# RWKV-7 delta-rule scan on one core: the sixth level of the triangular inverse on its 64x64 corner, in two row halves of the array, with one direction's key transposes in front of each half

## The chip, the cores and the metric

One core of a Trainium2 chip runs the whole kernel. The metric is device time in microseconds (us), the median over runs; lower is better. Times of single instructions come from one profiled execution.

## The reference

Two blocks of a network run in sequence over x of 1024 tokens and width 1024. The change lies in the first block's RWKV-7 branch: a gated delta rule, 16 heads of width 64, run forwards and backwards over 256 context tokens and 1024 tokens. Cut to what matters:

```python
def rwkv7_scan(r, w, k, v, kk, a, S0, reverse):
    def step(S, inp):
        sa = jnp.einsum('bhvk,bhk->bhv', S, kk_t)
        S = (S * w_t[:, :, None, :] - sa[..., None] * b_t[:, :, None, :]
             + v_t[..., None] * k_t[:, :, None, :])
        o = jnp.einsum('bhvk,bhk->bhv', S, inp[5])
        return S, o
    S, o = lax.scan(step, S0, xs, reverse=reverse)
...
    for d in (0, 1):                      # forwards and backwards
        S, o = rwkv7_scan(rh, w, kd, vh, kk, a, S0[d], reverse=(d == 1))
    o = head_norm((outs[0] + outs[1]), ln_w, ln_b, A_HEADS, A_GN_EPS) + bonus
    return ((o * silu(g)) @ w_o), states
```

## The kernel before

The function `rwkv` does the scan in chunks of 128 tokens. One chunk of one head needs the inverse of a 128x128 unit triangular matrix (the tokens of a chunk depend on one another through the keys). The work is cut into units `(i, n)`: `i` is one of 8 pairs of heads, `n` one of 5 pairs of chunks, so there are 40 units. A unit holds two directions, `x = 0` (forwards) and `x = 1` (backwards), and for each 4 matrices `q` (2 heads by 2 chunks). The four matrices of a direction lie side by side in one PSUM bank; direction `x` has banks `4x` to `4x+3`, `bank(x, 0)` to `bank(x, 3)`.

The inverse is built in levels. Y holds the inverse so far, block diagonal with blocks of 2^m after level m-1, and E the matrix that takes part in making the next factor. Level m of a direction:

- TensorE: `f` multiplies E by G (result F, in `bank(x, 0)`), and `ey` multiplies G by E and Y together (a moving operand of 256 columns, result in banks 1 and 2).
- VectorE: `join` takes F, multiplies it by the mask `lev{m}` and leaves the next G.
- ScalarE copies two of the four results of `ey` back to SBUF (`low{m}`), and the other two (`high{m}`) for x = 0; for x = 1 VectorE copies the `high{m}` ones.

Levels 1 to 4 are so done. Level 5 needs no new E: `f` makes F5 and `y_next` (`Y5`) makes the new Y alone, 128 columns wide. Level 6, the last, is `y_next` again (`Y6`) with G6 from F5. Its result lies only in a 64x64 corner of each 128x128 matrix, since the diagonal blocks of 64 are done by then: for x = 0 rows 0 to 63 and columns 64 to 127, for x = 1 the opposite corner. ScalarE copies Y5 and Y6 back (`y_out`, L1220).

Behind the levels of a unit the order on TensorE is written out by hand, and the next unit's front is interleaved with it: `turn_kv` (transposes of the next unit's keys and values, 4 instructions for each direction, L1299 and L1301, into `bank(x, 1)`; it waits for `low4`), `Y6`, `turn_ab` (4 transposes for each direction, L1310 and L1312, into `bank(x, 0)`; it waits for G6), `solve` (C0 = Y times the right side, L1347 on `b_Rr`; it waits for Y6's copy), `gram_b` (L1320 on `b_Bt`; it waits for `Btok`, ScalarE's copy of the transposes, L1201), `product` (L1347 on `b_C`), `gram_k` (L1320 on `b_Kt`), `refine` (L1347 on `b_G,b_EY`, eight in a row), `start` (L1338, L1341) and so on. `gram_b` and `gram_k` contract over 64 partitions only: their instructions go in turn to the upper and the lower 64 rows of the array, which the profile writes as `64*128`.

On ScalarE the copies stand in an order of their own, in which each waits for its turn: Y5 (x = 0, 1), the four copies of the keys and values (`keys_out`, L1195), Y6 (x = 0, 1), then `pairs_out` (L1200, L1201) and `solved` (L1224) of x = 0, and the same of x = 1.

Of the kernel before, what the change touches and what calls it, by code (L numbers as in the profile page):

```python
# [18 lines left out]
ALU = mybir.AluOpType  # L19
ACT = mybir.ActivationFunctionType  # L20
# [933 lines left out]
def rwkv(nc, G, proj, Xd, oa, v_tok, rope):  # L954
# [15 lines left out]
    with nc.cleanup_on_exit(), ExitStack() as ctx:  # L970
# [39 lines left out]
        by_head = lambda t: t.rearrange("p (t h c) -> p h t c", t=2, h=2)  # L1010
        spare = lambda h: bank(h, 3)
        both = lambda x: ps[:, 4 * x + 1:4 * x + 3].rearrange("p b (q a f) -> p (b q) a f", q=2, a=2)

# [9 lines left out]
        def level_names(n, x):  # L1023
            return {"pe": ["F0", "E0"] + sum(([f"F{m}", f"EY{m}"] for m in range(1, 5)), []) + ["F5", "Y5", "Y6"],
                    "act": ["E0"] + sum(([f"low{m}"] + ([] if high_on_dve(x) else [f"high{m}"]) for m in range(1, 5)), []) + ["Y5", "Y6"],
                    "dve": ["G0", "G1"] + sum(([f"G{m}"] + ([f"high{m - 1}"] if high_on_dve(x) and m < LEVELS - 1 else []) for m in range(2, LEVELS)), [])}
# [30 lines left out]
        with nc.Block() as block:  # L1057
# [124 lines left out]
            def _(act):  # L1182
# [34 lines left out]

                def y_out(i, n, x, m):
                    L[x]["pe"].wait(act, i, f"{n}.Y{m}")
                    L[x]["act"].done(A(Y[x], heads(x, 2), ACT.Copy), f"{n}.Y{m}")  # L1220

# [16 lines left out]
                for i, n in UNITS_B:  # L1238
                    nxt = after(i, n)
                    for m in range(1, 5):  # L1240
                        for x in range(2):
                            ey_out(i, n, x, m)
                    for x in range(2):
                        y_out(i, n, x, 5)
                    if nxt:
                        for x in range(2):
                            keys_out(*nxt, x)
                    for x in range(2):
                        y_out(i, n, x, last)
                    for x in range(2):  # L1250
# [19 lines left out]
            def _(pe):  # L1270
# [106 lines left out]

                def y_next(i, n, x, m):
                    L[x]["dve"].wait(pe, i, f"{n}.G{m}")
                    if m == 6:  # L1380
                        L[x]["act"].wait(pe, i, f"{n}.Y5")
                    L[x]["pe"].done(quad(bank(x, 2), Gs[x][m % 2], Y[x]), f"{n}.Y{m}")

                def levels(i, n):
                    for m in range(1, 6):
                        for x in range(2):
                            f(i, n, x, m)
                            if m < 5:
                                ey(i, n, x, m)
                            else:  # L1390
                                y_next(i, n, x, m)
                        if m == 1 and i and n == 0:
                            mean(i - 1)
                        if m == 1 and i and n == 1:
                            for x in range(2):
                                B[x]["dve"].wait(pe, i, "0.QT")
                            variance(i - 1)

                def solve(i, n, x):
# [86 lines left out]
                for i, n in UNITS_B:  # L1486
                    nxt = after(i, n)
                    levels(i, n)
                    if nxt:
                        turn_kv(*nxt, 0)  # L1490
                        turn_kv(*nxt, 1)
                    for x in range(2):
                        y_next(i, n, x, last)
                        if nxt:
                            turn_ab(*nxt, x)
# [26 lines left out]
            def _(dve):  # L1522
# [53 lines left out]
                def join(i, n, x, m):  # L1576
                    if m == 0:
                        F[x]["pe"].wait(dve, i, f"{n}.XT")
                    else:
                        L[x]["pe"].wait(dve, i, f"{n}.F{m - 1}")  # L1580
                    L[x]["dve"].done(V.tensor_tensor(Gs[x][m % 2][:], heads(x, 0 if m else 1), rep(K(f"lev{m}"), 4), ALU.mult), f"{n}.G{m}")  # L1581

# [1895 lines left out]
```

How the kernel before makes its waits and increments, by code:

```python
    def wait(self, back=0):  # L68
        self.eng.wait_ge(self.sem, self.it * self.per + (self.base + self.n - back))
# [48 lines left out]
    def load(self, eng, src, i, per, l, split=False):  # L118
        if split:
            eng.wait_ge(self.cut, i * per + (self.split_base + l + 1))
        else:
            eng.wait_ge(self.free, i * per + (self.base - self.split_base + l + 1))
        b = (self.base + l) % NBUF
        eng.dma_start(self.buf[:, b], src).then_inc(self.full[b], 16)
# [1 line left out]
    def landed(self, eng, i, per, l):  # L127
        n = self.base + l
        eng.wait_ge(self.full[n % NBUF], i * (16 * per // NBUF) + 16 * (n // NBUF + 1))
        return self.buf[:, n % NBUF]
# [1 line left out]
    def split_hi(self, act, l):  # L133
        n = self.split_base + l
        raw = self.landed(act, 0, 0, l)
        act.wait_ge(self.begun, n + 1)
        self.nc.scalar.activation(self.hl[:, n % NBUF, 0], raw, ACT.Copy).then_inc(self.hi_done, 1)
# [1 line left out]
    def split_lo(self, dve, l):  # L140
        n = self.split_base + l
        hi, lo = self.hl[:, n % NBUF, 0], self.hl[:, n % NBUF, 1]
        dve.wait_ge(self.hi_done, n + 1)
        self.nc.vector.tensor_tensor(lo, self.buf[:, (self.base + l) % NBUF], hi.bitcast(F32), ALU.subtract).then_inc(self.cut, 1)
# [1 line left out]
    def split_first(self, eng, scalar):  # L147
# [6 lines left out]
            self.nc.scalar.activation(hi, raw, ACT.Copy).then_inc(self.hi_done, 1)  # L154
        else:
            eng.wait_ge(self.hi_done, n + 1)
            self.nc.vector.tensor_tensor(lo, raw, hi.bitcast(F32), ALU.subtract).then_inc(self.cut, 1)
```

## Time and profile before

| | |
|---|---|
| time, median of 3 runs | 4689.36 us (4686.57 to 4690.65) |
| the profiled execution | 4687.34 us, of which 4685.6 us span from the first to the last instruction |
| TensorE matmuls | busy 4531.5 us (97%) |
| TensorE weight loads | busy 3671.8 us (78%) |
| VectorE | busy 2674.1 us (57%) |
| ScalarE | busy 1728.0 us (37%) |
| GpSimd | busy 457.7 us (10%) |
| granted TensorE clock, mean | 0.986 of 2.4 GHz |

Busy time counts an instruction from start to end, and the ends of matmuls overlap the next ones' starts: a matmul of 0.28 us can be followed by the next after 0.11 us. So what a group of matmuls costs is read from the start of the group to the start of the next group, not from its busy time. The scan's 40 units lie between 1373 and 2609 us of the span. In every unit the stretch that the change touches looks alike in the trace, so one unit is shown (i = 3, n = 2).

### The profile page before, as it was taken

The page shows a single profiled execution, that of the slowest core. Times are in us where ns is not written, and L with a number is a line of the kernel's source. Part 1 is how long each engine was busy: PE and PEld are TensorE (multiplying, and loading weights), DVE is VectorE, ACT ScalarE, POOL GpSimd, SP SyncE. Part 2 cuts the span into 40 slices and gives each one's busy share as a digit, 9 for nine tenths or more (in the row PEclk, how much of TensorE's full clock was granted, in tenths as well). Part 3 has the DMA queues.
Part 4 walks back from the last instruction along what each step waited for, and adds up shares of the span by engine and source line. Part 5 has one row for each costly group of instructions (what it writes and reads, how often), then busy time and mean ns, then how long its engine had stood idle before and what let it go on. Part 6 is the DMA issues. An engine that isn't in the chain of part 4 may idle for free. (4 is left out here: it accounts for less than half of the span.)

```text
span 4685.6 us, 66517 instructions
## 1 busy us (share of the span) xinstructions
PE 4531.5 (97%) x27608; PEld 3671.8 (78%) x27608; DVE 2674.1 (57%) x3938; ACT 1728.0 (37%) x2924; POOL 457.7 (10%) x371
## 2 busy tenths in 40 slices
PE   7999999999999999999999799899998789999999
PEld 4888877778999888988898444688777567888887
DVE  3245544555636676767677676546453755555543
ACT  3234444444424544554445343211343742111111
POOL 0000000000012233322334100000010000000000
PEclk8999999999999999999999999999999999999999
DMA  5244343434430110111012343333120021212222
GB/s 207 99 144 148 134 144 138 145 139 148 160 115 15 45 57 30 59 45 59 28 59 86 90 150 120 128 107 134 54 71 15 23 113 59 72 68 77 99 90 95
DMA packets 155978, 441.79 MB, mean 94 GB/s; under 512 B 17168, under 2 KB 47120, under 8 KB 140448
## 3 DMA queue, kind: packets, MB, share of 16 engines
q1 hardware_dynamic: 140624, 383.98, 23.5%
q0 software_dynamic: 9296, 32.58, 2.0%
q10 hardware_dynamic: 5760, 20.97, 1.2%
q8 instruction: 221, 3.62, 0.3%
q14 instruction: 77, 0.63, 0.0%
HBM read 294.86 MB, written 141.56 MB: 93 GB/s over the span
## 5 line engine op out<-in xcount | busy, mean ns | idle before, releaser
L202 PE MATMUL pr_ps<-uhl,w_split 128*128 128x512 f32 (+1 forms) x1520 | 586.9, 386 | 3.1 <-DVE w_split L145 2.2
L206 PE MATMUL pr_ps<-uhl,w_split 128*128 128x512 f32 (+1 forms) x1520 | 571.7, 376 | 0.0
L205 PE MATMUL pr_ps<-uhl,w_split 128*128 128x512 f32 (+1 forms) x1520 | 571.1, 376 | 0.0
L1581 DVE TENSOR_TENSOR b_G<-b_ps,cst 128x512 fp32r<-128x512 f32 x560 | 383.2, 689 | 95.4 <-PE b_ps L1361 93.7
L138 ACT ACTIVATE w_split<-share 128x2048 fp32r<-128x2048 f32 x64 | 122.6, 1916 | 698.9 <-DVE ou_vc L3303 271.1
L202 PEld LDWEIGHTS pr_ps<-uhl,w_split 128*128 128x128 f32 x1520 | 287.0, 189 | 81.7 <-issue 29.2
L205 PEld LDWEIGHTS pr_ps<-uhl,w_split 128*128 128x128 f32 x1520 | 287.3, 189 | 56.3 <-issue 5.8
L206 PEld LDWEIGHTS pr_ps<-uhl,w_split 128*128 128x128 f32 x1520 | 286.9, 189 | 52.8
L1124 POOL TENSOR_SCALAR b_Mr<-b_tri 128x512 fp32r<-128x512 f32 x80 | 117.8, 1490 | 1908.7 <-DVE b_tri L1565 1908.7
L202 PE MATMUL ou_ps<-ou_a,w_split 128*128 128x512 f32 x704 | 276.5, 393 | 7.7 <-DVE ou_a L2158 7.7
L1361 PE MATMUL b_ps<-b_G,b_EY 128*128 128x128 f32 x1600 | 275.4, 281 | 0.0
L206 PE MATMUL ou_ps<-ou_a,w_split 128*128 128x512 f32 x704 | 274.5, 390 | 0.0
L205 PE MATMUL ou_ps<-ou_a,w_split 128*128 128x512 f32 x704 | 274.5, 390 | 0.0
L776 DVE COPY pr_stage<-pr_ps 128x256 f32<-128x256 f32 (+1 forms) x92 | 49.7, 540 | 393.4 <-PE pr_ps L206 393.2
L1214 ACT ACTIVATE b_EY<-b_ps 128x512 fp32r<-128x512 f32 x320 | 192.1, 600 | 217.4 <-PE b_ps L1375 217.4
L202 PE MATMUL mx_ps<-mx_a,w_split 128*128 128x512 f32 x640 | 259.1, 405 | 13.5 <-DVE mx_a L2158 13.5
L205 PE MATMUL mx_ps<-mx_a,w_split 128*128 128x512 f32 x640 | 254.1, 397 | 0.0
L206 PE MATMUL mx_ps<-mx_a,w_split 128*128 128x512 f32 x640 | 253.9, 397 | 0.0
L1361 PEld LDWEIGHTS b_ps<-b_G,b_EY 128*128 128x128 f32 x1600 | 222.2, 189 | 36.8 <-issue 12.0
L202 PE MATMUL ou_ps<-ou_ext,w_split 128*128 128x512 f32 x576 | 224.1, 389 | 0.0
L205 PE MATMUL ou_ps<-ou_ext,w_split 128*128 128x512 f32 x576 | 224.1, 389 | 0.0
L206 PE MATMUL ou_ps<-ou_ext,w_split 128*128 128x512 f32 x576 | 224.1, 389 | 0.0
(498 smaller groups left out, 10030.2 us busy)
## 6 DMA issues: line engine op xcount, KB each, us to landing
w_ring<-in_w_in SPq DMA_DIRECT2D x41, 1024.0 KB, 5.3
proj<-pr_stage SPq DMA_DIRECT2D x160, 256.0 KB, 2.0
share<-in_w_up SPq DMA_DIRECT2D x24, 1024.0 KB, 4.8
ar<-share SPq DMA_DIRECT2D x32, 512.0 KB, 2.8
b_AR<-ar SPq DMA_DIRECT2D x64, 256.0 KB, 2.9
pr_raw<-proj SPq DMA_DIRECT2D x48, 256.5 KB, 3.5
ada<-in_ada_w SPq DMA_DIRECT2D x24, 512.0 KB, 5.6
ff<-ou_vc ACTq DMA_DIRECT2D x24, 512.0 KB, 2.6
```

The lines of the kernel that those rows point to most:

```text
L138: self.nc.scalar.activation(self.hl[:, n % NBUF, 0], raw, ACT.Copy).then_inc(self.hi_done, 1)
L202: mm = nc.tensor.matmul(dst, a[0], b[0], start=start, stop=False)
L205: nc.tensor.matmul(dst, a[0], b[1], start=False, stop=False)
L206: return nc.tensor.matmul(dst, a[1], b[0], start=False, stop=stop)
L776: V.tensor_copy(dst, src).then_inc(taken[1], 1)
L1124: F[x]["pool"].done(ts(Mr[x][:], tri[x][e][:], 1.0, None, ALU.mult), f"{n}.Mr")
L1214: L[x]["act"].done(A(EY[x][:, 0:2], both(x)[:, 0:2], ACT.Copy), f"{n}.low{m}")
L1361: mm = mmul(bank(x, 0)[:, q * P:(q + 1) * P], E[x][:, q] if m else Mr[x][:, q], Gs[x][m % 2][:, q], start=True, stop=True)
L1581: L[x]["dve"].done(V.tensor_tensor(Gs[x][m % 2][:], heads(x, 0 if m else 1), rep(K(f"lev{m}"), 4), ALU.mult), f"{n}.G{m}")
```

## The change

- Level 5's `f` no longer runs over the whole matrices. `y_five` makes Y5 for both directions first; then `corner_f` makes the corner of F5 alone: for each matrix a 64-row contraction, weights of 64 rows by 128 columns, moving operand of 64 rows by 64 columns. It alternates between the directions, and direction 0 lies in the upper 64 rows of the array (partitions), direction 1 in the lower.
- VectorE's last `join` becomes a multiplication by -1 of the 64x64 corners (64 partitions by 256 elements in place of 128 by 512), without the mask.
- `corner_y` takes the place of Y6: again 64-row contractions with 64 moving columns that alternate between the directions, now 0 in the lower rows and 1 in the upper. It begins with a wait for G6 and Y5's copy of both directions. ScalarE copies back the 64x64 corners alone (`corner_out`).
- `turn_kv` of x = 0 moves ahead of Y5, and `turn_kv` of x = 1 stands between `corner_f` and `corner_y`. The `turn_ab` of both directions stand behind `corner_y`, where x = 0's stood between the two Y6. On ScalarE `keys_out` is moved in the same way: x = 0's ahead of the Y5 copies, x = 1's behind them.
- The waits for `low4` and `high4` of a direction, which F5 had, are now those of its Y5; `turn_kv` has its wait for `low4` as before.

```diff
--- before.py
+++ after.py
@@ -1009,6 +1009,9 @@
         heads = lambda x, b: ps[:, 4 * x + b].rearrange("p (q f) -> p q f", q=4)
         by_head = lambda t: t.rearrange("p (t h c) -> p h t c", t=2, h=2)
         spare = lambda h: bank(h, 3)
+        edge = [slice(64, P), slice(0, 64)]
+        rest = [slice(0, 64), slice(64, P)]
+        corners = lambda x, b: bank(x, b)[:, 0:256].rearrange("p (q f) -> p q f", q=4)
         both = lambda x: ps[:, 4 * x + 1:4 * x + 3].rearrange("p b (q a f) -> p (b q) a f", q=2, a=2)
 
         last = LEVELS - 1
@@ -1021,7 +1024,7 @@
         high_on_dve = lambda x: x == 1
 
         def level_names(n, x):
-            return {"pe": ["F0", "E0"] + sum(([f"F{m}", f"EY{m}"] for m in range(1, 5)), []) + ["F5", "Y5", "Y6"],
+            return {"pe": ["F0", "E0"] + sum(([f"F{m}", f"EY{m}"] for m in range(1, 5)), []) + ["Y5", "F5", "Y6"],
                     "act": ["E0"] + sum(([f"low{m}"] + ([] if high_on_dve(x) else [f"high{m}"]) for m in range(1, 5)), []) + ["Y5", "Y6"],
                     "dve": ["G0", "G1"] + sum(([f"G{m}"] + ([f"high{m - 1}"] if high_on_dve(x) and m < LEVELS - 1 else []) for m in range(2, LEVELS)), [])}
 
@@ -1215,9 +1218,13 @@
                     if not high_on_dve(x):
                         L[x]["act"].done(A(EY[x][:, 2:4], both(x)[:, 2:4], ACT.Copy), f"{n}.high{m}")
 
-                def y_out(i, n, x, m):
-                    L[x]["pe"].wait(act, i, f"{n}.Y{m}")
-                    L[x]["act"].done(A(Y[x], heads(x, 2), ACT.Copy), f"{n}.Y{m}")
+                def y_out(i, n, x):
+                    L[x]["pe"].wait(act, i, f"{n}.Y5")
+                    L[x]["act"].done(A(Y[x], heads(x, 2), ACT.Copy), f"{n}.Y5")
+
+                def corner_out(i, n, x):
+                    L[x]["pe"].wait(act, i, f"{n}.Y6")
+                    L[x]["act"].done(A(Y[x][rest[x], :, edge[x]], corners(x, 2)[rest[x]], ACT.Copy), f"{n}.Y6")
 
                 def solved(i, n, x):
                     B[x]["pe"].wait(act, i, f"{n}.C0")
@@ -1240,13 +1247,14 @@
                     for m in range(1, 5):
                         for x in range(2):
                             ey_out(i, n, x, m)
+                    if nxt:
+                        keys_out(*nxt, 0)
                     for x in range(2):
-                        y_out(i, n, x, 5)
+                        y_out(i, n, x)
                     if nxt:
-                        for x in range(2):
-                            keys_out(*nxt, x)
+                        keys_out(*nxt, 1)
                     for x in range(2):
-                        y_out(i, n, x, last)
+                        corner_out(i, n, x)
                     for x in range(2):
                         if nxt:
                             pairs_out(*nxt, x)
@@ -1375,26 +1383,45 @@
                         mm = mmul(both(x)[:, q], Gs[x][m % 2][:, q], EY[x][:, q], start=True, stop=True)
                     L[x]["pe"].done(mm, f"{n}.EY{m}")
 
-                def y_next(i, n, x, m):
-                    L[x]["dve"].wait(pe, i, f"{n}.G{m}")
-                    if m == 6:
+                def y_five(i, n, x):
+                    L[x]["dve"].wait(pe, i, f"{n}.G5")
+                    L[x]["act"].wait(pe, i, f"{n}.low4")
+                    high(x).wait(pe, i, f"{n}.high4")
+                    L[x]["pe"].done(quad(bank(x, 2), Gs[x][1], Y[x]), f"{n}.Y5")
+
+                def corner_f(i, n):
+                    for q in range(4):
+                        for x in range(2):
+                            mm = mmul(corners(x, 0)[:, q], E[x][rest[x], q], Gs[x][1][rest[x], q, rest[x]], start=True, stop=True)
+                            if q == 3:
+                                L[x]["pe"].done(mm, f"{n}.F5")
+
+                def corner_y(i, n):
+                    for x in range(2):
+                        L[x]["dve"].wait(pe, i, f"{n}.G6")
                         L[x]["act"].wait(pe, i, f"{n}.Y5")
-                    L[x]["pe"].done(quad(bank(x, 2), Gs[x][m % 2], Y[x]), f"{n}.Y{m}")
+                    for q in range(4):
+                        for x in range(2):
+                            mm = mmul(corners(x, 2)[:, q], Gs[x][0][edge[x], q], Y[x][edge[x], q, edge[x]], start=True, stop=True)
+                            if q == 3:
+                                L[x]["pe"].done(mm, f"{n}.Y6")
 
                 def levels(i, n):
-                    for m in range(1, 6):
+                    for m in range(1, 5):
                         for x in range(2):
                             f(i, n, x, m)
-                            if m < 5:
-                                ey(i, n, x, m)
-                            else:
-                                y_next(i, n, x, m)
+                            ey(i, n, x, m)
                         if m == 1 and i and n == 0:
                             mean(i - 1)
                         if m == 1 and i and n == 1:
                             for x in range(2):
                                 B[x]["dve"].wait(pe, i, "0.QT")
                             variance(i - 1)
+                    for x in range(2):
+                        if x == 0 and after(i, n):
+                            turn_kv(*after(i, n), 0)
+                        y_five(i, n, x)
+                    corner_f(i, n)
 
                 def solve(i, n, x):
                     i_, n_ = before(i, n)
@@ -1487,11 +1514,10 @@
                     nxt = after(i, n)
                     levels(i, n)
                     if nxt:
-                        turn_kv(*nxt, 0)
                         turn_kv(*nxt, 1)
-                    for x in range(2):
-                        y_next(i, n, x, last)
-                        if nxt:
+                    corner_y(i, n)
+                    if nxt:
+                        for x in range(2):
                             turn_ab(*nxt, x)
                     solve(i, n, 0)
                     solve(i, n, 1)
@@ -1578,6 +1604,9 @@
                         F[x]["pe"].wait(dve, i, f"{n}.XT")
                     else:
                         L[x]["pe"].wait(dve, i, f"{n}.F{m - 1}")
+                    if m == last:
+                        L[x]["dve"].done(V.tensor_scalar(Gs[x][0][edge[x], :, rest[x]], corners(x, 0)[edge[x]], -1.0, None, ALU.mult), f"{n}.G{m}")
+                        return
                     L[x]["dve"].done(V.tensor_tensor(Gs[x][m % 2][:], heads(x, 0 if m else 1), rep(K(f"lev{m}"), 4), ALU.mult), f"{n}.G{m}")
 
                 def high_out(i, n, x, m):
```

TensorE's order behind the last `ey` (level 4) of a unit, the first one, before. `b_G` and `b_EY` hold G, and E with Y; `cst` is the identity of the transposes, `share` the memory in which this unit's keys lie; `128x128` is the moving operand's shape and x4 the count.

```order
L1375 MATMUL b_ps<-b_EY,b_G 128x256 x4
L1361 MATMUL b_ps<-b_G,b_EY 128x128 x4
L1347 MATMUL b_ps<-b_EY,b_G 128x128 x4
L1361 MATMUL b_ps<-b_G,b_EY 128x128 x4
L1347 MATMUL b_ps<-b_EY,b_G 128x128 x4
L1299 MATMUL b_ps<-cst,share 128x128 x2
...
L1347 MATMUL b_ps<-b_EY,b_G 128x128 x4
L1310 MATMUL b_ps<-cst,share 128x128 x2
L1312 MATMUL b_ps<-cst,share 128x128 x2
L1347 MATMUL b_ps<-b_EY,b_G 128x128 x4
```

The same place of the changed kernel, the lines with its own numbers (L1307 and L1309 are `turn_kv`, L1355 Y5, L1395 `corner_f`, L1405 `corner_y`, L1318 and L1320 `turn_ab`).

```order
L1383 MATMUL b_ps<-b_EY,b_G 128x256 x4
L1307 MATMUL b_ps<-cst,share 128x128 x2
L1309 MATMUL b_ps<-cst,share 128x128 x2
L1355 MATMUL b_ps<-b_EY,b_G 128x128 x8
L1395 MATMUL b_ps<-b_G,b_EY 128x64 x8
L1307 MATMUL b_ps<-cst,share 128x128 x2
L1309 MATMUL b_ps<-cst,share 128x128 x2
L1405 MATMUL b_ps<-b_EY,b_G 128x64 x8
L1318 MATMUL b_ps<-cst,b_AR 128x128 x2
L1320 MATMUL b_ps<-cst,share 128x128 x2
```

The eight instructions of F5 and the eight of Y6 became eight of 64 columns each, a group of transposes now stands ahead of Y5 and one between the two corner groups, and both `turn_ab` follow `corner_y`.

ScalarE's copies from level 4's last `low4` to the first `solved`, before:

```order
L1214 ACTIVATE b_EY<-b_ps 128x512
L1220 ACTIVATE b_EY<-b_ps 128x4x128 x2
L1195 ACTIVATE b_KV<-b_ps 128x256 x4
L1220 ACTIVATE b_EY<-b_ps 128x4x128 x2
L1200 ACTIVATE b_AM<-b_ps 128x4x64
L1201 ACTIVATE b_MB<-b_ps 128x4x64
L1224 ACTIVATE b_C<-b_ps 128x512
```

And now (L1217 is `low4`, L1223 Y5's copy, L1227 the corner's):

```order
L1217 ACTIVATE b_EY<-b_ps 128x512
L1198 ACTIVATE b_KV<-b_ps 128x256 x2
L1223 ACTIVATE b_EY<-b_ps 128x4x128 x2
L1198 ACTIVATE b_KV<-b_ps 128x256 x2
L1227 ACTIVATE b_EY<-b_ps 64x4x64 x2
L1203 ACTIVATE b_AM<-b_ps 128x4x64
L1204 ACTIVATE b_MB<-b_ps 128x4x64
L1231 ACTIVATE b_C<-b_ps 128x512
```

Two of the four key copies moved ahead of the Y5 copies, and the last pair of Y copies became smaller.

## Rows read from the trace of the kernel before

**Rows 1.** The scan's window: us; PE, PEld, DVE, ACT, POOL busy; PEclk; DMA; GB/s.

```profile
1373.20:2609.40 1236.20, 1231.32 (x12216) 1109.45 (x12216) 866.37 (x1621) 589.19 (x1252) 408.84 (x284) 1.00 0.14 48
```

**Rows 2.** Timeline of TensorE's matmuls in one unit: start, length, line, count.

```profile
1912.14 0.84 PE L1361 MATMUL b_ps<-b_G,b_EY 128*128 128x128 f32 x4
1912.81 0.61 PE L1347 MATMUL b_ps<-b_EY,b_G 128*128 128x128 f32 x4
1913.26 0.61 PE L1361 MATMUL b_ps<-b_G,b_EY 128*128 128x128 f32 x4
1913.70 0.61 PE L1347 MATMUL b_ps<-b_EY,b_G 128*128 128x128 f32 x4
1914.15 0.41 PE L1299 MATMUL b_ps<-cst,b_Kt 128*128 128x128 f32 x2
...
1914.97 0.64 PE L1347 MATMUL b_ps<-b_EY,b_G 128*128 128x128 f32 x4
...
1916.68 1.13 PE L1347 MATMUL b_ps<-b_Rr,b_EY 128*128 128x128 f32 x8
1917.74 2.14 PE L1320 MATMUL b_ps<-b_AR,b_Bt 64*128 64x256 f32 x16
1919.81 2.05 PE L1347 MATMUL b_ps<-b_C,b_tri 128*128 128x128 f32 x16
1921.79 2.00 PE L1320 MATMUL b_ps<-b_AR,b_Kt 64*128 64x256 f32 x16
1923.72 1.11 PE L1347 MATMUL b_ps<-b_G,b_EY 128*128 128x128 f32 x8
1924.66 0.39 PE L1338 MATMUL b_ps<-b_ident_r,b_Mr 128*128 128x128 f32 x2
```

**Rows 3.** Timeline of ScalarE in the same unit.

```profile
1911.89 0.59 ACT L1216 ACTIVATE b_EY<-b_ps 128x512 fp32r<-128x512 f32 x1
1912.37 0.60 ACT L1214 ACTIVATE b_EY<-b_ps 128x512 fp32r<-128x512 f32 x1
...
1914.85 1.21 ACT L1195 ACTIVATE b_KV<-b_ps 128x256 f32<-128x256 f32 x4
1915.90 1.20 ACT L1220 ACTIVATE b_EY<-b_ps 128x512 fp32r<-128x512 f32 x2
...
1917.53 0.62 ACT L1224 ACTIVATE b_C<-b_ps 128x512 f32<-128x512 f32 x1
...
1918.27 0.43 ACT L1201 ACTIVATE b_MB<-b_ps 128x256 f32<-128x256 f32 x1
```

**Rows 4.** Timeline of VectorE: the end of the same unit's levels.

```profile
1912.40 0.68 DVE L1585 CAST b_EY<-b_ps 128x512 fp32r<-128x512 f32 x1
1913.01 0.69 DVE L1581 TENSOR_TENSOR b_G<-b_ps,cst 128x512 fp32r<-128x512 f32 x1
1913.90 0.69 DVE L1581 TENSOR_TENSOR b_G<-b_ps,cst 128x512 fp32r<-128x512 f32 x1 [0.20 <-PE b_ps L1361]
```

**Rows 5.** Timeline of VectorE later in the unit: two operations of 256 elements.

```profile
1925.38 0.41 DVE L1593 TENSOR_TENSOR b_WN<-b_C,b_ps 128x256 f32<-128x256 f32 x1
1925.70 0.42 DVE L1594 SCALAR_TENSOR_TENSOR b_WN<-b_ps,b_C 128x256 f32<-128x256 f32 x1
```

**Rows 6.** Timeline of VectorE in the unit before: operations of 64 elements.

```profile
1901.01 0.48 DVE L1607 TENSOR_SCALAR b_S<-b_ps,b_dmp 128x64 f32<-128x64 f32 x2 [1.02 <-PE b_ps L1462]
```

**Rows 7.** Timeline of weight loads: half-array ones, 1917.74 to 1917.86.

```profile
1917.74 0.30 PEld L1320 LDWEIGHTS b_ps<-b_AR,b_Bt 64*128 64x128 f32 x4
```

**Rows 8.** Timeline of weight loads: whole-array ones, and the one that waited.

```profile
1913.20 0.53 PEld L1361 LDWEIGHTS b_ps<-b_G,b_EY 128*128 128x128 f32 x4
...
1918.74 0.73 PEld L1320 LDWEIGHTS b_ps<-b_AR,b_Bt 64*128 64x128 f32 x8 [0.27 <-ACT b_MB L1201]
```

**Rows 9.** Groups by line in the scan: count, busy us, mean ns of one.

```profile
L1220 ACT ACTIVATE b_EY<-b_ps 128x512 fp32r<-128x512 f32 x160 | 95.8, 609 | 31.5 <-PE b_ps L1347 31.5
...
L1446 PE MATMUL b_ps<-b_WN,b_MB 128*64 128x64 f32 x576 | 37.5, 222 | 0.0
```

## The prediction

> **What bounds the kernel now.** I read the window of the scan first: in 1236.2 us TensorE's matmuls are busy for 1231.3 us, at a granted clock of 1.00 (2.4 GHz), while VectorE is busy for 866 and ScalarE for 589 [rows 1]. So the scan goes at TensorE's pace, and what a unit loses or gains between the starts of TensorE's groups is the kernel's loss or gain. ScalarE makes two Y5 and two Y6 copies a unit, 160 in all, so there are 40 units [rows 9]; 39 of them have a next unit whose transposes are interleaved.
>
> Then the timeline of TensorE. F5 of x = 0 starts at 1912.14, F5 of x = 1 at 1913.26, and each Y5 and the second F5 take 0.44 to 0.45 us from start to start, 0.11 us for a matmul. The first F5 took 0.67: 0.22 us of waiting. The eight transposes of both `turn_kv` take 1914.15 to 1914.97 = 0.82 us (0.41 for a direction; the `turn_ab` are of the same kind), and `solve` starts at 1916.68 [rows 2]. From F5 to `solve` a unit spends 4.54 us, all of it touched by the change.
>
> Two more waits lie behind. `gram_b` of x = 1 waited: its weight load at 1918.74 had a hole of 0.27 us before it and follows ScalarE's `Btok`, which ended at 1918.27 + 0.43 = 1918.70 [rows 3, 8]. Its price: `gram_b` takes 1917.74 to 1919.81 = 2.07 us and `gram_k`, the same work without the wait, 1921.79 to 1923.72 = 1.93, so 0.14. And `solve` takes 1.06 us to the next start, where `refine`, eight matmuls too, takes 0.94 [rows 2]; of the 0.12, some 0.09 are the switch to half-array instructions (below), and 0.03 a wait for Y6's copy of x = 1, which ended at 1915.90 + 1.20 = 1917.10 [rows 3]. Both waits are ScalarE's queue being late.
>
> **What the parts cost.** Removed: 16 whole-array matmuls, 16 x 0.11 = 1.78 us. Added: 16 half-array ones. G, E and Y are fp32r, as the copies that write them show [rows 3, 4]; the half-array instructions of the trace work on plain f32. So I bound the price of a pair (one in each half). The half-array weight loads of `gram_b`: four, two for each half, take 0.30 us in all [rows 7], where four whole-array loads take 0.53 [rows 8]. With 0.19 for the length of one, that is 0.11 from pair to pair against 0.11 from load to load. So the halves load side by side, and a pair costs 0.11 us if the weights set the pace; if the halves took turns in this format it would be 0.22. I take 0.11, since the load has the same 128 columns: four pairs in 0.44 us where eight matmuls took 0.89.
>
> Switches. The change goes from whole to half and back twice more in each unit. `product`, 16 whole-array matmuls, takes 1.98 us to `gram_k` against 16 x 0.1115 = 1.78, so 0.20 for the switch with the first load laid bare; `refine` takes 0.94 against 0.89, so 0.05 for a bare first load in the scan's number format, with no switch behind it [rows 2]. Left for the switch itself: 0.10 to 0.15; I take 0.10, hence 0.15 with the load. Above the row the Trainium skill ("TensorEngine Tiling (Array Packing)", Key Properties) speaks against this change: changing the tiling mode drains the array. The trace agrees, with those 0.10 us; were a switch free, the two that lie on the path here would give back 2 x 0.15 x 39 = 12 us more than I forecast.
>
> Handovers: a copy starts 0.03 us after the recorded end of the matmul (F5 of x = 1 ends at 1913.26 + 0.61 = 1913.87, VectorE starts at 1913.90 [rows 2, 4]); a weight load follows a copy by 0.05 (1918.70 to 1918.74 [rows 3, 8]).
>
> **The new sequence**, in the times of this unit:
> - `turn_kv` of x = 0 starts at 1912.14 and ends its slot at 1912.55. It fills the wait that F5 had: `high4` of x = 0 ends at 1911.89 + 0.59 = 1912.48 [rows 3], so Y5 of x = 0 loads at 1912.53 and is through at 1912.53 + 0.05 + 0.45 = 1913.03.
> - Y5 of x = 1 now needs `high4` of x = 1, VectorE's copy of 1912.40 + 0.68 = 1913.08 [rows 4]. Before, that was hidden behind Y5 of x = 0. It loads at 1913.13: a new wait of 0.10 and a bare load of 0.05. Its slot ends at 1913.63.
> - Switch: `corner_f` loads at 1913.73; its fourth pair starts at 1913.73 + 0.05 + 3 x 0.11 = 1914.11 and its record ends 0.22 later (a matmul of 64 columns, [rows 9]), at 1914.33.
> - VectorE makes G6 of x = 0 from 1914.36. 256 elements for each partition take 0.41, the next begins 0.33 later [rows 5]: x = 1 ends at 1914.36 + 0.33 + 0.41 = 1915.10. Below this lies the row of 64 elements, two in 0.48 [rows 6]: 1914.84; above it the full-length 0.69 with 0.61 between starts [rows 4]: 1915.66.
> - Meanwhile `turn_kv` of x = 1 runs and ends at about 1914.75, so 0.3 us of TensorE lie idle, and both switches around the transposes are hidden in them.
> - `corner_y` loads at 1915.15, its fourth pair starts at 1915.53. ScalarE's queue isn't what it waits for: the keys' copies of x = 0 start when `low4` of x = 1 is through (1912.97), take 0.27 each, and two Y5 copies of 0.6 end by 1914.6.
> - Switch, bare load, 0.82 us of `turn_ab`: 1915.53 + 0.05 (its own 64 columns, an estimate) + 0.15 + 0.80 (0.82 less the bare load that is counted already) = 1916.53 is `solve`'s start. Before it was 1916.68: **0.15 us gained.**
> - ScalarE has the two corner copies (256 elements: 0.4 each, 0.27 apart, as the keys' copies: four in 1.21 [rows 3]) from 1915.78 to 1916.45, not 1917.10. So `solve` of x = 1 finds Y6 there: **0.03 gained.** The first C0 copy, which started at 1917.53 because the queue was late, starts when its matmuls are through: 1916.53 + 0.03 + 0.33 + 0.28 + 0.03 = 1917.20. `Btok` of x = 1, which ended 1.17 after that start, ends at 1918.37, while `gram_b` now starts at 1917.74 - 0.18 = 1917.56 and asks for it at about 1918.40 (half of `gram_k`'s 1.93 less one load of 0.11 after its start): **0.14 gained.**
>
> Nothing further behind loses it again: VectorE's masks and GpSimd's copies start from `gram_b` and move with it. Sum: 0.32 us a unit, 39 x 0.32 = 12.5 us. The last unit has no transposes to fill the wait for G6 and loses an estimated 0.5. Total 12.0: the profiled execution would come to 4687.3 - 12.0 = 4675.3, and the median, 2.0 above it, to 4689.4 - 12.0 = **4677.4 us**.
>
> So the 0.9 us of matmul time taken away come to 0.32, since the path now runs through Y5, a switch, the corner, VectorE and the second corner.
>
> **The rivals.**
> - *The halves take turns (slower).* A pair costs 0.22 in this number format; both corner groups are on the path, each 0.44 longer. Against it: the loads of [rows 7] overlap. For it: all half-array instructions of the trace are of the other format. The unit then changes by +0.88 - 0.32 = +0.56, 39 of them +22 us, with the last one 4712. It decides where a pair costs over 0.15 (8 pairs x 0.04 = 0.32).
> - *Something on the new path costs a little more (no change to be seen).* The two bare switches at 0.15 instead of 0.10, or semaphores that take 0.05 longer at three places, or the wait for `high4` longer: 0.2 us a unit, 8 us. For it: the path is a chain of seven handovers, each priced from other places. 4685.
> - *G6 full length.* VectorE's price doesn't follow the elements: 0.56 later, 39 x 0.56 = 22 us, 4699. Against it: 0.41 for 256 elements in [rows 5].
> - *G6 short, or pairs quicker.* By [rows 6] G6 ends 0.26 sooner: -10 us, 4667. TensorE would then have no idle time left, so more isn't to be had there.
>
> **How the numbers follow.** Forecast (4671 to 4683) 0.60; a little more costly 0.18; halves in turn 0.10; full-length G6 0.03; short 0.09. About 0.2% (9.4 us) is what a measurement of this kernel tells from no change, so faster begins at 4680. Of the forecast's case three quarters are below that (0.45), and all of the short one (0.09): faster 0.54. Same: 0.15 and 0.16 of the second case, 0.31. Slower: 0.10 + 0.03 + 0.02 = 0.15. The range reaches from the short G6 with a little more, 4665, to the full-length one, 4699; only the halves in turn are outside.
>
> **What would show it.** From the first `turn_kv` to `solve` 4.4 us in a unit, not 4.5; weight loads of `corner_f` in pairs 0.01 apart and 0.11 from pair to pair; a hole of some 0.3 us before `corner_y` that VectorE's G6 ends; no hole before `gram_b` of x = 1; the 40 units' window 12 us shorter. I am wrong if the pairs start 0.1 apart, if ScalarE's Y5 copy ends the wait of `corner_y`, or if the wait before `gram_b` is still there.

## The result, and the profile after

The changed kernel takes **4731.02 us** (median of 5 runs, 4721.81 to 4734.12) against 4686.57 (4685.37 to 4690.65) before, where two runs more have joined the three of the table: a ratio of 1.0091, 95% interval 1.0079 to 1.0103. It is slower by 44 us, where 12 us faster was forecast, and it lies outside the range. The profiled execution of the changed kernel took 4721.81 us with a span of 4720.0. It is the fastest of the five, so the profile shows the loss at its mildest.

The busy times of the whole page show nothing of this:

```profile
PE 4543.8 (96%) x27608; PEld 3672.3 (78%) x27608; DVE 2657.5 (56%) x3938; ACT 1719.6 (36%) x2924; POOL 458.1 (10%) x371
```

One stretch inside the scan does. The columns are those of [rows 1]; the first row is the kernel before, the second the changed one, in fences of their own.

```profile
1400.00:2580.00 1180.00, 1175.83 (x11672) 1059.18 (x11671) 828.54 (x1549) 564.21 (x1201) 384.75 (x266) 1.00 0.14 48
```

```profile
1400.00:2580.00 1180.00, 1155.40 (x11317) 1026.72 (x11313) 787.76 (x1502) 540.66 (x1165) 357.67 (x248) 0.97 0.14 46
```

The reader is to see two things. The granted clock is 0.97, where it was 1.00: 3% of 1180 us are some 35 us. And TensorE is idle for 25 us of the stretch, where it was idle for 4. Windows of 5 us in the changed kernel show where the clock went:

```profile
1405.00:1410.00 5.00, 5.00 (x39) 4.66 (x40) 4.54 (x8) 3.49 (x7) 0.00 (x0) 1.00 0.01 3
1410.00:1415.00 5.00, 4.42 (x43) 3.85 (x41) 2.49 (x5) 3.77 (x9) 0.00 (x0) 0.98 0.00 0
1415.00:1420.00 5.00, 5.00 (x25) 4.63 (x26) 0.00 (x0) 3.05 (x8) 0.00 (x0) 0.50 0.02 3
1420.00:1425.00 5.00, 5.00 (x38) 4.11 (x36) 3.88 (x6) 0.00 (x0) 2.98 (x2) 0.83 0.00 0
```

The second window holds an idle time of 0.58 us (4.42 of 5.00 busy). Behind it the clock is at 0.50, the lower of its two levels (1.2 GHz), comes back in the fourth window and is 1.00 until it falls again some units later (0.50 in 1545 to 1550). The timeline of TensorE around the same place, columns as in [rows 2]:

```profile
1413.42 0.38 PE L1309 MATMUL b_ps<-cst,share 128*128 128x128 f32 x2
1414.38 0.66 PE L1405 MATMUL b_ps<-b_EY,b_G 64*128 64x64 f32 x8 [0.58 <-DVE b_G L1608]
1414.97 0.69 PE L1318 MATMUL b_ps<-cst,b_AR 128*128 128x128 f32 x2
1415.45 0.64 PE L1320 MATMUL b_ps<-cst,share 128*128 128x128 f32 x2
...
1416.59 1.95 PE L1355 MATMUL b_ps<-b_Rr,b_EY 128*128 128x128 f32 x8
```

The pairs of `corner_y` (L1405) still go nearly at full speed; the transposes behind them take 0.64 for two instead of 0.38, and `solve` 1.95 instead of 1.09. The hole is the wait for G6, VectorE's two copies of F5's corner. It is there in every unit, and the clock falls behind about every fourth of them: ten times in the stretch, each time within 1 us of the end of a hole.

Apart from the clock, the path is no shorter either. A unit with its clock at 1.00, from `solve` to `solve`, takes 31.57 us before (from 1916.68 [rows 2]) and 31.70 after (from 1931.94, below). Two of every five units are shorter (30.89 and 29.83 before), and they too are 0.13 longer now. The next `solve` in the timeline of the kernel before, and in that of the changed one:

```profile
1948.25 1.14 PE L1347 MATMUL b_ps<-b_Rr,b_EY 128*128 128x128 f32 x8
```

```profile
1963.64 1.09 PE L1355 MATMUL b_ps<-b_Rr,b_EY 128*128 128x128 f32 x8
```

The timeline of the changed kernel's TensorE over such a unit's end:

```profile
1927.08 0.41 PE L1307 MATMUL b_ps<-cst,b_Kt 128*128 128x128 f32 x2
1927.33 0.38 PE L1309 MATMUL b_ps<-cst,b_V 128*128 128x128 f32 x2
1927.57 1.23 PE L1355 MATMUL b_ps<-b_EY,b_G 128*128 128x128 f32 x8
1928.73 0.63 PE L1395 MATMUL b_ps<-b_G,b_EY 64*128 64x64 f32 x8
1929.30 0.44 PE L1307 MATMUL b_ps<-cst,b_Kt 128*128 128x128 f32 x2
1929.57 0.38 PE L1309 MATMUL b_ps<-cst,b_V 128*128 128x128 f32 x2
1930.53 0.63 PE L1405 MATMUL b_ps<-b_EY,b_G 64*128 64x64 f32 x8 [0.58 <-DVE b_G L1608]
1931.10 0.44 PE L1318 MATMUL b_ps<-cst,b_AR 128*128 128x128 f32 x2
...
1931.94 1.09 PE L1355 MATMUL b_ps<-b_Rr,b_EY 128*128 128x128 f32 x8
1932.96 2.00 PE L1328 MATMUL b_ps<-b_AR,b_Bt 64*128 64x256 f32 x16
1934.89 2.05 PE L1355 MATMUL b_ps<-b_C,b_tri 128*128 128x128 f32 x16
```

From the first `turn_kv` to `solve` it takes 4.86 us; the stretch from F5 to `solve` that it answers to took 4.54 [rows 2], and 4.39 was forecast. `gram_b` now takes 1.93 (1932.96 to 1934.89), not 2.07: the wait before its x = 1 is gone, as forecast.

### The profile page after: what moved, and what is told of

It reads as the page before. It is cut to its first block and busy times, and to the rows that moved or that the text cites. A ratio compares the mean times of both kernels' runs of the same rounds, so it can differ in the third digit from the quotient of the medians.

```text
span 4720.0 us, 66517 instructions
## 1 busy us (share of the span) xinstructions
PE 4543.8 (96%) x27608; PEld 3672.3 (78%) x27608; DVE 2657.5 (56%) x3938; ACT 1719.6 (36%) x2924; POOL 458.1 (10%) x371
## 5 line engine op out<-in xcount | busy, mean ns | idle before, releaser
L1610 DVE TENSOR_TENSOR b_G<-b_ps,cst 128x512 fp32r<-128x512 f32 x480 | 328.0, 689 | 87.2 <-PE b_ps L1369 85.7
L1217 ACT ACTIVATE b_EY<-b_ps 128x512 fp32r<-128x512 f32 x320 | 192.4, 601 | 217.4 <-PE b_ps L1383 217.4
L1383 PE MATMUL b_ps<-b_EY,b_G 128*128 128x256 f32 x1280 | 220.1, 293 | 0.0
L1369 PE MATMUL b_ps<-b_G,b_EY 128*128 128x128 f32 x1280 | 217.6, 280 | 0.0
```

The lines of the kernel that those rows point to most:

```text
L1217: L[x]["act"].done(A(EY[x][:, 0:2], both(x)[:, 0:2], ACT.Copy), f"{n}.low{m}")
L1369: mm = mmul(bank(x, 0)[:, q * P:(q + 1) * P], E[x][:, q] if m else Mr[x][:, q], Gs[x][m % 2][:, q], start=True, stop=True)
L1383: mm = mmul(both(x)[:, q], Gs[x][m % 2][:, q], EY[x][:, q], start=True, stop=True)
```

## The experiments

Each edit is against the changed kernel. The clock is that of the stretch 1400 to 2580, the unit that of the timeline at full clock. The kernel before had medians of 4685.16, 4686.32 and 4686.65 us beside the three sets of runs.

**`fill_t`: the hole filled.** Four more transposes stand in front of `corner_y`, into a bank that is free there. They are extra work that nothing uses. Theory A: the clock falls because TensorE idles before `corner_y`. Theory B: it falls for another reason, the half-array instructions for one.

```diff
                         turn_kv(*nxt, 1)
+                        F[0]["act"].wait(pe, nxt[0], f"{nxt[1]}.Vtok")
+                        for q in range(4):
+                            tp(bank(0, 1)[:, q * P:(q + 1) * P], Kt[i % 2][0][:, (at(0, n) + q % 2) * P:(at(0, n) + q % 2 + 1) * P], K("ident"))
                     corner_y(i, n)
```

> Four more key transposes (whole array, results unused) stand in the wait before corner_y, 0.43 us of work in a hole of 0.58 us, off the path. Theory H (the clock falls because TensorE stands still for 0.6 us in every unit): the hole shrinks to 0.15 us, the scan's granted clock goes from 0.97 to 1.00, and the time falls by some 30 to 38 us, to 4692 to 4700. Theory W (what counts is real multiplying work; transposes and 64-column half-array instructions are too thin): the clock stays at 0.97 and the time within 10 us of the changed kernel's 4731. Theory M (all of the loss is mis-sized steps of the path, no clock): same time, 4731, too.

Measured: 4695.73 us, 1.0022 [1.0013, 1.0032]; clock 1.00; unit 31.70, so the extra work lengthened nothing. The clock is back and with it 35 us; the hole left is 0.14 us. A stands against B, though the added work could matter as well as the closed hole.

```profile
1400.00:2580.00 1180.00, 1170.94 (x11776) 1044.31 (x11777) 805.62 (x1538) 554.88 (x1197) 379.45 (x263) 1.00 0.14 48
```

**`fill_m`, `fill_f`: other work in the hole.** The same place; first four fp32r matmuls of E and G5 (`fill_m`), then two f32 matmuls with the identity, each of which is two instructions in the trace (`fill_f`). Unused work too, behind the same wait as in `fill_t`.

```diff
+                        for q in range(4):
+                            mmul(bank(0, 1)[:, q * P:(q + 1) * P], E[0][:, q], Gs[0][1][:, q], start=True, stop=True)
```

```diff
+                        for q in range(2):
+                            mmul(bank(0, 1)[:, q * P:(q + 1) * P], K("ident"), Kt[i % 2][0][:, (at(0, n) + q) * P:(at(0, n) + q + 1) * P], start=True, stop=True)
```

> The same place and length, but four real whole-array fp32r matmuls of 128 columns (E times G5, results unused) in place of the transposes. H and W both: clock back to 1.00 in the scan and 4692 to 4700. Where fill_t stays slow and this one doesn't, W holds against H. M: 4731.

> The hole before corner_y filled as in fill_t and fill_m, now with two real whole-array f32 matmuls (identity times the keys), four instructions of 0.11 us. fill_t's transposes of f32 data kept the clock up (4695.7), fill_m's fp32r matmuls only in part (4707.3). If f32 operands are what keeps the array busy enough: as fill_t, 4692 to 4698. If transposing is: as fill_m, 4703 to 4712.

Measured: `fill_m` 4707.3, 1.0053 [1.0038, 1.0068], unit 31.70, clock 0.99, fallen at some four places; `fill_f` 4696.6, 1.0021 [1.0011, 1.0031], 31.70, clock 1.00.

```profile
1400.00:2580.00 1180.00, 1170.04 (x11684) 1047.19 (x11685) 799.84 (x1527) 550.66 (x1187) 376.56 (x260) 0.99 0.14 48
```

TensorE is as busy here (1170.04 us) as with the transposes (1170.94), and the clock is not held as well. So idle time alone seems not to be the whole rule: what fills the hole counts too. It is not that transposes count more, since plain f32 matmuls hold the clock as they do. One difference besides the number format is left: the hole that remains is 0.18 us in `fill_m`, 0.14 in `fill_t` and 0.13 in `fill_f`. No run separates the two.

**`kv_late`: the transposes of both directions between the corners.**

```diff
                     for x in range(2):
-                        if x == 0 and after(i, n):
-                            turn_kv(*after(i, n), 0)
                         y_five(i, n, x)
...
                     if nxt:
+                        turn_kv(*nxt, 0)
                         turn_kv(*nxt, 1)
```

ScalarE's `keys_out` of x = 0 moves behind the Y5 copies in the same way (not shown).

> Both directions' key transposes stand between corner_f and corner_y, as they stood before Y6 in the kernel before; nothing ahead of Y5. Y5 of x = 0 waits 0.4 us for its last copy instead, but the path (high4 of x = 1, Y5, corner_f, G6, corner_y) is the same: units of 31.70 us where the clock is full. The hole before corner_y shrinks from 0.58 to 0.15. If the clock falls by the thin stretch behind Y5 alone: clock 1.00, 4692 to 4700. If it goes by idle time wherever it lies in the unit: 4721 to 4734.

Measured: 4694.28, 1.0017 [1.0008, 1.0026]; unit 31.70; clock 1.00. The stretch, and TensorE's timeline:

```profile
1400.00:2580.00 1180.00, 1158.10 (x11607) 1028.95 (x11602) 806.49 (x1539) 561.36 (x1197) 380.56 (x263) 1.00 0.14 48
```

```profile
1910.22 1.23 PE L1354 MATMUL b_ps<-b_EY,b_G 128*128 128x128 f32 x8 [0.35 <-ACT b_EY L1219]
1911.39 0.63 PE L1394 MATMUL b_ps<-b_G,b_EY 64*128 64x64 f32 x8
...
1913.18 0.63 PE L1404 MATMUL b_ps<-b_EY,b_G 64*128 64x64 f32 x8
1914.60 1.09 PE L1354 MATMUL b_ps<-b_Rr,b_EY 128*128 128x128 f32 x8
```

This is the cleanest comparison of the study: the same instructions, the same path (31.70), no added work. Of the hole of 0.58, 0.35 now lie before Y5 and 0.14 before `corner_y`. TensorE is idle for 22 us of the stretch, hardly less than the changed kernel's 25 and more than `fill_m`'s 10, and yet the clock holds. The 37 us from here to the changed kernel (4731.0 less 4694.3) are the clock's; the 8 us from the kernel before to here are the path's, as far as the units show it (0.13 us each). To fill the wait before Y5 with transposes, as the changed kernel does, brings nothing on the path: the unit is 31.70 either way.

**`kv_late_hole`: a hole put back.** The edit of `kv_late`, and on top of it VectorE makes G6 of x = 0 twice, first into a scratch tile that nothing reads.

```diff
                     if m == last:
+                        if x == 0:
+                            V.tensor_scalar(scr[edge[x]], corners(x, 0)[edge[x]], -1.0, None, ALU.mult)
```

> kv_late (4694.3, clock 1.00) with one more VectorE operation ahead of G6 of x = 0: it reads the corner once more into a spare tile, so that G6 of both comes about 0.45 us later and the hole before corner_y grows from 0.15 to about 0.6 us, as in the changed kernel, but with both groups of transposes in front of the hole. Path: 0.4 to 0.45 us a unit, 16 to 18 us, 4710 to 4712. If a hole of 0.6 us beside half-array work brings the clock down: 25 to 35 us more, 4735 to 4747. If the transposes' place is what mattered: 4710 to 4712 and the clock stays.

Measured: 4707.9, 1.0047 [1.0032, 1.0062]; unit 32.05; clock 1.00.

```profile
1919.77 1.24 PE L1355 MATMUL b_ps<-b_EY,b_G 128*128 128x128 f32 x8 [0.35 <-ACT b_EY L1220]
...
1923.08 0.63 PE L1405 MATMUL b_ps<-b_EY,b_G 64*128 64x64 f32 x8 [0.48 <-DVE b_G L1609]
```

Two holes, together 0.83 us a unit, more than the 0.58 of the changed kernel, and the clock holds. The sum of the idle time in a unit does not decide. Here a single hole of 0.48 does not let it fall; one of 0.58 in the changed kernel does. That the length makes this difference is not shown: the transposes of both directions stand in front of the hole here, those of one direction there, and no run has this order with a hole of 0.58.

**`order`: the change's order alone, level 6 on the whole array.**

```diff
                 def corner_f(i, n):
-                    for q in range(4):
-                        for x in range(2):
-                            mm = mmul(corners(x, 0)[:, q], E[x][rest[x], q], Gs[x][1][rest[x], q, rest[x]], start=True, stop=True)
-                            if q == 3:
-                                L[x]["pe"].done(mm, f"{n}.F5")
+                    for x in range(2):
+                        L[x]["pe"].done(quad(bank(x, 0), E[x], Gs[x][1]), f"{n}.F5")
```

and so for `corner_y`, `join` (with its mask again) and the copy of Y6 (not shown).

> The change's order alone: F5 and Y6 over the whole matrices, VectorE's and ScalarE's last steps full length, transposes and waits where the change puts them. Path by the rows: Y5, F5 x = 0 and x = 1, G6 of x = 1 full length (0.69), Y6: solve 0.2 to 0.4 us later than before, 4695 to 4702. H: the hole before Y6 is at most 0.2 us, clock 1.00. W: whole-array work, clock 1.00. M: the same. A time near 4731 would say that the order alone, not the corner, brings the clock down.

Measured: 4719.1, 1.0074 [1.0057, 1.009]; unit 32.32; clock 1.00.

```profile
1926.29 1.08 PE L1355 MATMUL b_ps<-b_EY,b_G 128*128 128x128 f32 x8 [0.68 <-DVE b_G L1601]
```

So the order costs 0.75 us a unit (32.32 against 31.57), and the corners give back 0.62 (31.70): the corners are worth having, the order isn't. And with a hole of 0.68, longer than the changed kernel's, the clock holds. How long a hole the clock bears depends on more than its length; what differs here are the instructions around it.

**`order_hole`: `order` with a longer hole**, by an extra, unused VectorE operation ahead of G6 of x = 0.

```diff
+                    if m == last and x == 0:
+                        V.tensor_scalar(scr[:], heads(x, 0)[:, :, 0:64], -1.0, None, ALU.mult)
                     L[x]["dve"].done(V.tensor_tensor(Gs[x][m % 2][:], heads(x, 0 if m else 1), rep(K(f"lev{m}"), 4), ALU.mult), f"{n}.G{m}")
```

> order (4719.1, clock 1.00 in the levels, hole of 0.68 us before Y6, all whole-array work) with one more VectorE operation of 256 elements ahead of G6: the hole grows to 1.0 to 1.1 us. Path: 0.33 to 0.45 us a unit, 13 to 18 us, 4732 to 4737. If idle time alone decides above some length between 0.6 and 1 us: clock falls, 4757 to 4772. If half-array work is needed for it: 4732 to 4737.

Measured: 4775.34, 1.0187 [1.0164, 1.0209]; unit 32.66 where the clock is full, 34.4 where it fell, which is in most units; clock 0.96.

```profile
1445.90 0.38 PE L1310 MATMUL b_ps<-cst,share 128*128 128x128 f32 x2
1447.29 1.58 PE L1356 MATMUL b_ps<-b_EY,b_G 128*128 128x128 f32 x8 [1.01 <-DVE b_G L1604]
1448.67 0.65 PE L1319 MATMUL b_ps<-cst,b_AR 128*128 128x128 f32 x2
```

With 1.01 us of idle time the whole-array order loses its clock too. Half-array instructions are not needed for a fall.

**`wide`: half-array corners with 128 moving columns** instead of 64, in `corner_f` and in `corner_y`; the half of each product that isn't needed is not used.

```diff
-                            mm = mmul(corners(x, 0)[:, q], E[x][rest[x], q], Gs[x][1][rest[x], q, rest[x]], start=True, stop=True)
+                            mm = mmul(heads(x, 0)[:, q], E[x][rest[x], q], Gs[x][1][rest[x], q], start=True, stop=True)
```

> corner_f and corner_y with 128 moving columns in place of 64, still in the two row halves; the copies read the same corners. The weight loads set the pace (0.11 us a pair), so the path and the hole of 0.58 us stay. Theory C (the clock falls because the stretch around the hole streams too few columns; the order run kept its clock with a hole of 0.68 us and whole-array work): clock back to 1.00 for most of the scan, 4692 to 4705. Theory R (half of the rows idle is what counts, or hole and half rows together): columns don't help, 4721 to 4734.

Measured: 4715.28, 1.0062 [1.0047, 1.0077]; unit 31.75; clock 0.99, fallen at five or six places.

```profile
1926.17 0.66 PE L1405 MATMUL b_ps<-b_EY,b_G 64*128 64x128 f32 x8 [0.58 <-DVE b_G L1608]
```

The same hole of 0.58, twice the columns around it, and the clock falls about half as often. Twice the columns cost 0.05 us a unit: a pair is paced by its weight loads, not by its columns.

**`g6_act`: G6 of x = 1 on ScalarE**, so that the two copies of F5's corner run side by side.

```diff
+                def corner_neg(i, n, x):
+                    L[x]["pe"].wait(act, i, f"{n}.F5")
+                    L[x]["act"].done(A(Gs[x][0][edge[x], :, rest[x]], corners(x, 0)[edge[x]], ACT.Copy, scale=-1.0), f"{n}.G6")
...
-                        L[x]["dve"].wait(pe, i, f"{n}.G6")
-                        L[x]["act"].wait(pe, i, f"{n}.Y5")
+                        L[x]["act"].wait(pe, i, f"{n}.G6" if x else f"{n}.Y5")
+                    L[0]["dve"].wait(pe, i, f"{n}.G6")
```

The edit has a second part: `corner_y` now has three waits instead of four, and the one for VectorE's G6 stands last.

> G6 of x = 1 is made by ScalarE, beside VectorE's G6 of x = 0, and corner_y waits for three semaphores instead of four. The step from corner_f to corner_y loses VectorE's second copy (0.46 us) and one wait (0.05): the hole shrinks from 0.58 to about 0.1, a unit gets 0.45 to 0.5 us shorter: 18 to 20 us. H: the clock returns as well, 31 to 38 us more, in all 4673 to 4682, faster than the kernel before. W: work per time rises only a little, the clock stays low in part: 4690 to 4713. M: 4711.

Measured: **4672.75, 0.9973 [0.9962, 0.9983]**; unit 31.14; clock 1.00. The stretch, and the timeline of VectorE, ScalarE and the weight load at that place:

```profile
1400.00:2580.00 1180.00, 1175.69 (x11858) 1047.16 (x11857) 807.88 (x1532) 576.45 (x1253) 395.58 (x275) 1.00 0.14 48
```

```profile
1905.42 0.43 DVE L1615 TENSOR_SCALAR b_G<-b_ps 64x256 fp32r<-64x256 f32 x1 [1.38 <-PE b_ps L1400]
1905.45 0.38 ACT L1227 ACTIVATE b_G<-b_ps 64x256 fp32r<-64x256 f32 x1
...
1905.96 0.33 PEld L1410 LDWEIGHTS b_ps<-b_EY,b_G 64*128 64x128 f32 x4 [0.23 <-issue]
```

Both copies run within 0.43 us; `corner_y` starts 0.54 after the first of them, not 1.10. Of these 0.56 us, 0.45 are the copies side by side (they end at 1905.85, 0.43 after the first one's start and not 0.88) and 0.11 the handover (the load follows by 0.11, not 0.22), which the waits bring, as the next experiment shows. TensorE's order and work are those of the changed kernel here, with nothing added; only the hole before `corner_y` is closed, to 0.02 us, and the clock is back. Of the 58 us to the changed kernel, 0.56 us a unit are 22, and the 36 that remain agree with the 37 of `kv_late`. The version is faster than the kernel before by 0.27% and has both the shorter path and the clock.

**`waits`, `fewer_waits`: the semaphore waits.** `waits` is `fill_t` with the two waits for Y5 ahead of the two for G6. `fewer_waits` is `g6_act` with one of the three waits taken from each Y5, one that another wait on the same semaphore covers: `low4` for x = 0, G5 for x = 1.

```diff
                     for x in range(2):
-                        L[x]["dve"].wait(pe, i, f"{n}.G6")
                         L[x]["act"].wait(pe, i, f"{n}.Y5")
+                    for x in range(2):
+                        L[x]["dve"].wait(pe, i, f"{n}.G6")
```

> fill_t (4695.7) with corner_y's four waits in another order: both of Y5's copies first, which are long done, then both of G6. The load of corner_y came 0.225 us behind the end of G6 of x = 1; two of the four waits stood behind the one that comes last but one. If each wait that follows costs TensorE's queue about 0.05 us, the handover falls to 0.12 to 0.17 and the time by 2 to 4 us, 4692 to 4694. If the handover is a fixed price of a half-array load after idle time, nothing changes: 4695.7.

> g6_act (4672.8) with two waits instead of three in front of each Y5: the one left out is implied by another on the same semaphore. Y5 of x = 1 loaded 0.115 us behind the end of its last copy. If each wait instruction on TensorE's queue costs about 0.05 us behind the last release: 0.05 us a unit, 2 us, 4670.8. If the waits ahead of the last one are worked off while it waits: nothing, 4672.8.

Measured: `waits` 4690.3, 1.001 [1.0001, 1.002], unit 31.59 against `fill_t`'s 31.70; `fewer_waits` 4671.81, 0.9969 [0.9957, 0.998], unit 31.14 as `g6_act`. VectorE and the weight load of `waits`:

```profile
1911.27 0.88 DVE L1612 TENSOR_SCALAR b_G<-b_ps 64x256 fp32r<-64x256 f32 x2 [1.37 <-PE b_ps L1395]
...
1912.26 0.55 PEld L1406 LDWEIGHTS b_ps<-b_EY,b_G 64*128 64x128 f32 x8 [0.24 <-issue]
```

VectorE ends at 1912.15, the load follows 0.11 later. In the changed kernel it followed 0.22 later. A wait that is long fulfilled costs 0.11 us when it stands behind the one that comes last. Ahead of it, it costs nothing that shows: Y5 of x = 1 loads 0.115 us behind its last copy with three waits and with two.

**`b_early`: the `b` transposes in front of `corner_y`**, on top of `g6_act`: they go between the corners, into another bank, with their copies moved up in ScalarE's order (not shown).

```diff
                         turn_kv(*nxt, 1)
+                        for x in range(2):
+                            turn_b(*nxt, x)
                     corner_y(i, n)
```

> g6_act (4672.8) with the next unit's four transposes of B moved from behind corner_y to in front of it, into a bank that is free there, and their copies to the time in which ScalarE is idle. They fill what is left of the hole (0.15 us) and bring Btok forward, so that turn_ab is 0.41 us instead of 0.82. If the hole is all there is to win: 0.1 to 0.15 us a unit, 4667 to 4669. If gram_b of x = 1 had been waiting for Btok too: up to 4 us more, 4663. If TensorE has no idle time there: 4672.8.

Measured: 4676.53, 0.9979 [0.997, 0.9989]; unit 31.27, 0.13 more than `g6_act`. After `g6_act` no hole is left to fill, so work moved there pushes `corner_y` back: it starts 3.24 us after the first `turn_kv`, where it was 2.89. Behind it only half of the transposes are left, and they no longer cover ScalarE's copy of the corners, for which `solve`'s weight load now waits:

```profile
1910.24 0.97 PEld L1376 LDWEIGHTS b_ps<-b_Rr,b_EY 128*128 128x128 f32 x8 [0.20 <-ACT b_EY L1235]
```

## Why the prediction was wrong, by its own steps

**The hole.** "So 0.3 us of TensorE lie idle, and both switches around the transposes are hidden in them": this is the step that failed. The idle time was costed at nothing, since it lay inside a gain that was already counted. It measured 0.58, and it took TensorE's clock: 37 us of the 44. No rival had this mechanism. The trace of before gave no warning of it, since TensorE idles there for 4 us in 1180; but that is itself the warning: the clock of 1.00 had never been seen with a hole of this kind in it.

The Trainium skill ("TensorE: Matmul & The Clock Gate", Part 4: PE-mode transpose) states of transposes, which it times for bf16, that they don't count as work for the clock in the same way as matmuls. By that, `fill_t` should have helped less than the plain matmuls of `fill_f`, or not at all; it gave back 35 us and the clock of 1.00, and `fill_f` no more (4695.7 and 4696.6 us). The runs decide: here f32 transposes hold the clock.

**The path.** Forecast 0.32 us less a unit, measured 0.13 more at full clock. In microseconds after the first `turn_kv`, forecast and measured (1927.08 is the zero of the measured ones):

| step | forecast | measured |
|---|---|---|
| Y5 of x = 1 loads | 0.99 | 1.06 |
| `corner_f` starts | 1.59 | 1.65 |
| G6 of x = 0 starts | 2.22 | 2.32 |
| G6 of x = 1 ends | 2.96 | 3.20 |
| `corner_y` loads | 3.01 | 3.42 |
| `solve` starts | 4.39 | 4.86 |

ScalarE was no part of it: it had its Y5 copies done at 1929.44, 1.1 us before `corner_y`. The timelines of ScalarE, of VectorE and of the weight loads of the changed kernel:

```profile
1928.31 1.13 ACT L1223 ACTIVATE b_EY<-b_ps 128x512 fp32r<-128x512 f32 x2
```

```profile
1929.40 0.88 DVE L1608 TENSOR_SCALAR b_G<-b_ps 64x256 fp32r<-64x256 f32 x2 [1.38 <-PE b_ps L1395]
```

```profile
1928.73 0.52 PEld L1395 LDWEIGHTS b_ps<-b_G,b_EY 64*128 64x128 f32 x8
...
1930.50 0.55 PEld L1405 LDWEIGHTS b_ps<-b_EY,b_G 64*128 64x128 f32 x8 [0.79 <-DVE b_G L1608]
```

- *Y5 of x = 1.* Its load follows VectorE's copy of `high4` by 0.115, where 0.05 was taken for every handover. 0.07 too little.
- *Pairs.* Right: eight loads in 0.52 us, so a pair costs 0.11 and the halves run side by side. The rival of halves in turn is out.
- *The bare switch.* Right: from the load of Y5 of x = 1 to that of `corner_f` 0.59, forecast 0.60, with 0.10 for the switch. But "2 x 0.15 x 39 = 12 us" for a free switch counts the bare load too; with 0.10 it is 8.
- *The end of `corner_f`.* "Its record ends 0.22 later": a half-array matmul of 64 columns has a record of 0.274 us. 0.05 too little.
- *G6.* "The next begins 0.33 later": the two, each 0.42 long, take 0.88 together, so they start 0.46 apart and don't overlap. 0.13 too little. This was read from two operations of another kind [rows 5].
- *The handover to `corner_y`.* "A weight load follows a copy by 0.05" was read from one load that waited for ScalarE. This one has four waits, the last of them long fulfilled, and follows by 0.22. 0.17 too little; `waits` gave 0.11 of it back by order alone.
- *Behind.* `corner_y` to `solve` 1.44, not 1.38, so 0.06 too little. (0.82 less a bare load of 0.05 is 0.77, where the sum has 0.80; with 0.77 it would be 0.09.) The gains after `solve` came as forecast: from +0.32 at `solve` (4.86 against 4.54) to +0.13 in the whole unit is 0.19, against 0.17 forecast.

The small misses come to 0.47 at `solve`. The rival "something on the new path costs a little more" names the mechanism, "a chain of seven handovers, each priced from other places", but priced it at 0.2. Over 39 units +0.13 is 5 us, and the last unit, without transposes to fill the wait, loses 0.9 where 0.5 was estimated (31.36 against 30.45). Together some 6 us; `kv_late` measures 8, and the other 2 aren't accounted for.

**What stays open** is what exactly the clock asks for. The runs tell only this: whole-array order, holes of 0.68 held and 1.01 not; half-array order, 0.48 held (with both groups of transposes in front) and 0.58 not, though less often with 128 columns than with 64; a hole filled down to 0.14 us with f32 work is as good as none, down to 0.18 with fp32r work not quite. Nor is it known why the fall comes behind some of the equal holes and not the others.

## What to carry to other kernels

When a change opens an idle time on a TensorE that ran without one, read the granted clock by windows behind it, not its mean (0.97), and count the hole as a risk for all that follows, even when the path pays for it already. If a hole can't be closed, move independent work into it; here that alone was worth 37 us, more than any step of the change. In a chain of handovers, split two equal copies over two engines (0.45 us a unit here) and place the wait that comes last at the end (0.11).

## What the runs showed of the hardware that was not expected

- Half the clock behind a hole of 0.58 us in a scan that was otherwise busy, behind about every fourth of equal holes.
- Idle time can be had in two pieces, 0.35 and 0.48 us a unit, at a clock of 1.00 throughout.
- Four fp32r matmuls of 128 columns in a hole held the clock less well than f32 transposes or matmuls of the same length: 0.99 against 1.00, 11 us; the hole left was 0.18 against 0.14.
- A fulfilled wait behind the last one costs 0.11 us before a weight load; one ahead of it costs nothing that could be measured.
- Half-array pairs of 128 moving columns cost hardly more than those of 64: 0.05 us for the eight pairs of a unit.
